# Attention in a fused decoder layer: first scores between the halves of the last projection, softplus ahead of the output's parts

## The chip, the core and the metric

The kernel runs on one core of a Trainium2 chip, as one launch. The time is device microseconds of one execution; before the change the median of three runs is 1053.36 us (1053.25 to 1054.24). In the tables and texts PE is TensorE (matmuls), PEld its weight loads, DVE is VectorE, ACT is ScalarE and SP is SyncE, which issues the DMAs. Every engine takes its own instructions in order and meets the others through semaphores.

## The reference

One decoder layer over 512 tokens of 1024 values, all in float32: a first SwiGLU, the token mixer, a second SwiGLU, a gated per-layer embedding, each with its norms. The change is in the mixer:

```
proj = h @ w_in
# eight stick-breaking heads
z = q k^T / 8
log_1m_beta = where(causal, log_sigmoid(-z), 0)
tail = reverse exclusive cumsum of log_1m_beta over the keys
a = where(causal, exp(log_sigmoid(z) + tail), 0);  o_sb = a v
# eight forgetting heads
logits = q k^T / 8 + F[t] - F[s], causal;  w = softmax(logits);  o_fx = w v
merged = concat(rms_norm(o_sb), rms_norm(o_fx))
out = merged @ w_out
```

## The kernel before

Each float32 operand is split into a rounded high part (made by ACT, `_hi`) and a rest (made by DVE as value minus high part, `_lo`), and a product is three matmuls: `product`, lines 1758 to 1760.

The mixer works in four tiles. Tile j holds one stick-breaking head pair and one forgetting head pair; each half-tile `hh` computes one head of each kind, number `hd = 2j + hh`. Tiles 0 to 2 are one loop body (`more` true), tile 3 is written out after it (`more` false). While tile j is computed, TensorE also projects the six columns (q, k, v of both kinds) of tile j + 1: `project(0)`, `project(1)`, `project(2)` in each half-tile, each in two weight units of twelve matmuls. All of them accumulate in one PSUM bank, `G_BANK` (bank 4). DVE empties it with `project_out` into `hold` (line 1427), and the next `project` waits for that (`hold_ready`). The second half-tile's `project(2)` is the last one of the tile.

A half-tile has, on TensorE: `first_logits` (lines 2064 to 2071) into banks 5 and 6; in the first half `v_transpose(0)` and `v_transpose(1)` (line 2019, four transposes each, into banks 7 and 3); the triangular sums on `sp_r`, 20 matmuls (line 2100), which wait for `sp_lo`; the last logits block `logits(1)`, which waits for the first softmax exponential (`p_exp`), since it reuses bank 5; `weigh(0)` (line 2115), the weights' transposes (line 2133), `weigh(1)`. `first_scores` (lines 2010 and 2013) computes z of the head that comes next.

From z, `softplus` goes three times over (ACT Abs, Exp, Ln; DVE line 1447), then ACT rounds (line 853) and DVE takes the rest (line 1453), which gives `sp_lo`. `qk_split` makes high and low parts of q and k (ACT lines 833 and 834, DVE lines 1433 and 1436); SP doubles the k rows by a DMA after it, and `first_scores` waits for that. `v_split` rounds v out of banks 7 and 3 (ACT line 838, DVE line 1441). `unit(x)` is one weight unit's split in the loop (ACT line 611, DVE line 1110); in tile 3 it is `part_out`: tile 3 has no projection of a next tile and instead multiplies the output weights with the three finished tiles, eight rows r of the output in `parts(x)`. Row r = 0 and row r = 2 both go through bank 4: row 2 waits until row 0 is out of it (`BANK4_FREE`, semaphore `part_lo`, ACT line 895 and DVE line 1508). Row 1 goes through bank 7 and waits for `v_split` to have read it.

`out_copy` and `out_sum` put the two halves of a head's output together (lines 942 and 1570), `out_hi` and `out_lo` round it and add its square (lines 949, 952, 1577, 1142).

The order on each engine is written by hand, in `mixer_tile` of each engine.

Of the kernel before, what the change touches and what calls it, by code (L numbers as in the profile page):

```python
# [32 lines left out]
TILES = HEADS // 2  # L33
# [146 lines left out]
def build(nc, t, out):  # L180
# [7 lines left out]
    with ExitStack() as ctx:  # L188
# [411 lines left out]
        def _(act):  # L600
# [235 lines left out]
            def v_split(tile, kind):  # L836
                act.wait_ge(v_t, 2 * tile + kind + 1)
                act.activation(v_r[kind][:, :, :, 0, :], v_source(kind), ACT.Copy).then_inc(v_hi, 1)
# [48 lines left out]
            def mixer_tile(j, more):  # L887
                for hh in range(2):
                    hd = 2 * j + hh

                    def part_out(x):
                        for r, b in zip(PART_AT[hh][x // 2], PART_BANKS[hh][x // 2]):
                            if r < EVICTED:
                                act.wait_ge(w_used, U_OUT + r + 1)
                                act.activation(xg[:, 0, PART_ROW[r], :], bank[b][:, :], ACT.Copy).then_inc(part_hi, 1)
                            if (hh, x) != (1, 2):
                                ahead(U_OUT, 0, 0, r)

                    def unit(x):
                        if more:  # L900
                            ahead(U_MIX + TILE_UNITS, j, TILE_UNITS, 6 * hh + x)
                        elif x % 2 == 0:
                            part_out(x)

                    def softmax_exp(i, b):
                        lb, at, w = L_AT[b]
                        src = L_BANKS[lb % 2][:, at:at + w]
                        first = 512 * lb + at

                        act.wait_ge(neg_max, 4 * hd + (1, 3, 3, 4)[i])  # L910
                        act.activation(pr[:, first:first + w], src, ACT.Exp, bias=stat[:, 0, b:b + 1],
                                       accum_out=stat[:, 1, b:b + 1]).then_inc(p_exp, 1)
                    if hh == 0:
                        v_split(j, 0)
                        v_split(j, 1)
                        if not more:
                            unit(0)
                    for i, b in enumerate((3, 2, 0)):
                        softmax_exp(i, b)
                    if hh == 1 and more:  # L920
                        unit(0)
                        unit(1)
                    act.wait_ge(tri_done, hd + 1)
                    for b in range(3):
                        c = slice(512 * b, 512 * b + Z_W[b])
                        act.activation(el[:, c], Z[b][:, 0:Z_W[b]], ACT.Exp).then_inc(a_exp, 1)
                        act.wait_ge(a_exp, 3 * hd + b + 2)
                        act.activation(sp_r[0][:, c], el[:, c], ACT.Copy).then_inc(a_hi, 1)
                    softmax_exp(3, 1)
                    if hh == 0 and more:  # L930
                        unit(0)
                        unit(1)
                    if hh == 1 and not more:
                        unit(0)
                    unit(2)
                    unit(3)
                    if hh == 1 and more:
                        qk_split(j + 1, 0)

                    def out_copy(kind):  # L940
                        act.wait_ge(o_done, 2 * hd + kind + 2)
                        act.activation(o_sum[halves[hh], kind, :], O_BANK[halves[0], :], ACT.Copy).then_inc(o_half, 1)

                    def out_hi(kind, gain):
                        if hh == 0:
                            return
                        act.wait_ge(o_added, 2 * hd + kind + 2)
                        g = gains[:, ds(GAIN_AT[gain] + j, 1)]
                        act.activation(oT[0][:, ds(j + 4 * kind, 1), :], o_sum[:, kind, :].unsqueeze(1), ACT.Copy,
                                       scale=g).then_inc(o_hi, 1)  # L950
                        act.wait_ge(added, ADD_AT[N_SB] + 2 * j + kind)
                        act.activation(o_sq, o_sum[:, kind, :], ACT.Square).then_inc(squared, 1)
                    out_copy(0)
                    for b in range(3):
                        c = slice(512 * b, 512 * b + Z_W[b])
                        act.wait_ge(pt_done, 3 * hd + b + 1)
                        act.activation(pt_r[0][:, c], PT_BANKS[b][:, 0:Z_W[b]],
                                       ACT.Copy).then_inc(pt_hi, 1)
                    if hh == 0:
                        softplus(hd + 1)  # L960
                        unit(4)
                        unit(5)
                        out_copy(1)
                    else:
                        if more:
                            qk_split(j + 1, 1)
                            unit(4)
                        out_hi(0, "sb_group_g")
                        if not more:
                            for r in PART_AT[1][1] + PART_AT[1][2]:  # L970
                                ahead(U_OUT, 0, 0, r)
                        unit(5)
                        out_copy(1)
                        if more:
                            softplus(hd + 1)
                        out_hi(1, "fox_group_g")


# [127 lines left out]
        def _(dve):  # L1106
# [392 lines left out]
            def mixer_tile(j, more):  # L1499
                for hh in range(2):  # L1500
# [38 lines left out]
                        dve.tensor_scalar(pr[:, c], pr[:, c], stat[:, 2, b:b + 1], None, MUL).then_inc(p_scaled, 1)  # L1539
                    if hh == 0:  # L1540
                        v_split(j, 0)
                        v_split(j, 1)
                        if not more:
                            unit(0)
                    for i, b in enumerate((3, 2, 0)):
                        normalise(i, b)
                    if hh == 1 and more:
# [4 lines left out]
                    for b in range(3):  # L1552
                        c = slice(512 * b, 512 * b + Z_W[b])
                        dve.wait_ge(a_hi, 3 * hd + b + 1)
                        dve.tensor_tensor(sp_r[1][:, c], el[:, c], plain(sp_r[0][:, c]), SUB).then_inc(a_lo, 1)
                    normalise(3, 1)
                    if hh == 0 and more:
                        unit(0)
                        unit(1)
                    if hh == 1 and not more:  # L1560
                        unit(0)
                    unit(2)
                    project_out(1)
                    unit(3)
                    if hh == 1 and more:
                        qk_split(j + 1, 0)

                    def out_sum(kind):
                        dve.wait_ge(o_half, 2 * hd + kind + 1)
# [17 lines left out]
                    if hh == 0:  # L1587
# [5 lines left out]
                        unit(4)  # L1593
                        unit(5)
                        out_sum(1)
                    else:
                        if more:
                            qk_split(j + 1, 1)
                            unit(4)
                        project_out(2)  # L1600
                        out_lo(0, "sb_group_g")
                        if not more:
                            for r in PART_AT[1][1] + PART_AT[1][2]:
                                ahead(U_OUT, 0, 0, r)
                        unit(5)
                        out_sum(1)
                        if more:
                            for b in range(3):
                                softplus(hd + 1, b)
                            softplus_lo(hd + 1)  # L1610
                        out_lo(1, "fox_group_g")


# [141 lines left out]
        def _(pe):  # L1755
# [266 lines left out]
            def mixer_tile(j, more):  # L2022
                for hh in range(2):
# [16 lines left out]
                    def parts(x):  # L2040
                        if more:
                            return
                        for r, b in zip(PART_AT[hh][x], PART_BANKS[hh][x]):
                            pe.wait_ge(w_lo, U_OUT + r + 1)
                            if b == 7:
                                pe.wait_ge(v_lo, 2 * TILES)
                            if b == 0:
                                pe.wait_ge(a_exp, 3 * hd + 2)
                            if r == 0:
# [30 lines left out]
                    if not more:  # L2080
                        first_logits()
                    project(0)
                    parts(0)
                    if more:
                        first_logits()
                    if hh == 0:
                        pe.wait_ge(hold_ready, 6 * j + 4)
                        pe.wait_ge(o_added, 2 * hd + 1)
                        v_transpose(0)
                        v_transpose(1)  # L2090

                    pe.wait_ge(sp_lo, 3 * hd + 3)
                    for c in range(TB):
                        b, at, w = Z_AT[c]
                        for jc in range(c, TB):
# [3 lines left out]
                            for part in range(2):  # L2099
                                last = pe.matmul(Z[b][:, off:off + jw], lhs, sp_r[part][:, 512 * jb + jat:512 * jb + jat + jw],  # L2100
                                                 start=False, stop=(jc == TB - 1 and part == 1), skip_group_check=True)
                    last.then_inc(tri_done, 1)

                    pe.wait_ge(p_exp, 4 * hd + 1)
                    logits(1).then_inc(l_done, 1)
                    project(1)
                    parts(1)

# [26 lines left out]
                        last.then_inc(pt_done, 1)  # L2135
                    if hh == 0:
                        first_scores(j, 1)
                    project(2)
                    parts(2)
                    pe.wait_ge(pt_lo, 3 * hd + 3)  # L2140
                    pe.wait_ge(o_added, 2 * hd + 2)
                    weigh(1, pt_r)
                    if hh == 1 and more:
                        first_scores(j + 1, 0)

            pe.wait_ge(consts, 1)
            keep_busy(14, bank[0])
# [149 lines left out]
```

## Time and profile before

| | us |
|---|---|
| median of three runs | 1053.36 |
| lowest, highest | 1053.25, 1054.24 |
| the profiled execution | 1053.56 |
| its span | 1051.7 |
| PE busy (with modelled ends) | 1038.6 |
| DVE busy | 785.5 |
| ACT busy | 558.4 |
| tiles 0 to 3 in the span | about 398 to 599 |

The profile is one execution. The gap of 1.9 us between its own time and its span lies outside the span. Matmuls overlap, so TensorE's cost is read best from start to start, and idle time in front of an instruction stands in square brackets with what ended it. The mean granted TensorE clock of the execution is 0.997 of full speed.

### The profile page before, as it was taken

To read this page: it belongs to the slowest core of one execution; us is meant where nothing else is said; L and a number is where in the kernel's file an instruction comes from. 1 tells how busy PE (TensorE), PEld (TensorE's weight loads), DVE (VectorE), ACT (ScalarE), POOL (GpSimd) and SP (SyncE) were. 2 spreads that over 40 slices of the span, in tenths; PEclk is the share of its full clock that TensorE was granted. 3 is DMA by queue.
4 is the path that set the end of the run, shared out by engine and by line. 5 is a ranking of instruction groups with operands and counts; after the bars stand their busy time and mean duration, and the time that the engine had idled before them with its cause. 6 is when DMAs were issued, how large, how long until landed. Compare 5 with 4: busy or idle time off the path is not lost.

```text
span 1051.7 us, 16615 instructions
## 1 busy us (share of the span) xinstructions
PE 1038.6 (99%) x6118; PEld 923.7 (88%) x6118; DVE 785.5 (75%) x1107; ACT 558.4 (53%) x922; POOL 10.0 (1%) x33
## 2 busy tenths in 40 slices
PE   9999999999999999999999999999999999999997
PEld 7889999998888878888888888889999998888886
DVE  6889888864343789796969889899888865454655
ACT  6634444343333558686869846544444344344645
POOL 1000000000002000000000000000000000000000
PEclk9999999999999999999999999999999999999999
DMA  6353423303323233232312122263423305444002
GB/s 213 94 175 106 135 81 106 98 21 111 95 94 100 61 100 90 62 88 58 85 51 61 56 85 81 83 188 108 134 81 105 97 21 162 144 135 159 1 21 80
DMA packets 99948, 100.59 MB, mean 96 GB/s; under 512 B 6672, under 2 KB 82192, under 8 KB 99888
## 3 DMA queue, kind: packets, MB, share of 16 engines
q1 hardware_dynamic: 99472, 99.47, 31.2%
q8 instruction: 40, 0.66, 0.3%
q10 hardware_dynamic: 416, 0.30, 0.1%
q14 instruction: 20, 0.16, 0.1%
HBM read 94.44 MB, written 2.10 MB: 92 GB/s over the span
## 4 chain that ended last, share of the span: by engine, by line
PE 87%; DVE 6%; ACT 4%; issue 2%; DMA 0%; DVEq 0%; ACTq 0%
PE bank L1758 27%; PE bank L1759 27%; PE bank L1760 27%; PE bank L2100 2%; DVE w_r L1110 1%; PE bank L2115 1%; DVE scratch L1656 1%; ACT scratch L847 0%; DVE big L1436 0%; DVE big L1453 0%; PE bank L2064 0%; ACT scratch L845 0%; DVE big L1433 0%; DMA gains<-in_gains 0%; DVE acc L1130 0%
## 5 line engine op out<-in xcount | busy, mean ns | idle before, releaser
L1110 DVE TENSOR_TENSOR w_r<-w_raw,w_r 128x512 fp32r<-128x512 f32 x204 | 138.0, 688 | 134.2 <-ACT w_r L611 128.6
L1758 PE MATMUL bank<-big,w_r 128*128 128x512 f32 (+1 forms) x676 | 236.1, 349 | 0.1
L1759 PE MATMUL bank<-big,w_r 128*128 128x512 f32 (+1 forms) x676 | 235.1, 348 | 0.0
L1760 PE MATMUL bank<-big,w_r 128*128 128x512 f32 (+1 forms) x676 | 235.0, 348 | 0.0
L611 ACT ACTIVATE w_r<-w_raw 128x512 fp32r<-128x512 f32 x204 | 125.3, 627 | 182.4 <-PE bank L1760 179.1
L1758 PE MATMUL bank<-big,xg 128*128 128x256 f32 (+1 forms) x728 | 214.2, 294 | 0.0
L1760 PE MATMUL bank<-big,xg 128*128 128x256 f32 (+1 forms) x728 | 213.7, 294 | 0.0
L1759 PE MATMUL bank<-big,xg 128*128 128x256 f32 (+1 forms) x728 | 213.7, 293 | 0.0
L666 ACT ACTIVATE xg<-over 128x1024 fp32r<-128x1024 f32 x72 | 75.4, 1055 | 143.4 <-DVE over L1199 90.0
L1758 PE MATMUL bank<-xg,w_r 128*128 128x512 f32 x378 | 150.1, 397 | 0.6 <-DVE scratch L1427 0.6
L1759 PE MATMUL bank<-xg,w_r 128*128 128x512 f32 x378 | 147.4, 390 | 0.0
L1760 PE MATMUL bank<-xg,w_r 128*128 128x512 f32 x378 | 147.3, 390 | 0.0
L1758 PEld LDWEIGHTS bank<-big,w_r 128*128 128x128 f32 x676 | 128.0, 189 | 17.0 <-DVE big L1577 0.6
L1760 PEld LDWEIGHTS bank<-big,w_r 128*128 128x128 f32 x676 | 128.0, 189 | 16.1
L1759 PEld LDWEIGHTS bank<-big,w_r 128*128 128x128 f32 x676 | 128.0, 189 | 15.9 <-issue 0.2
L1760 PEld LDWEIGHTS bank<-big,xg 128*128 128x128 f32 x728 | 139.5, 192 | 2.9
L1759 PEld LDWEIGHTS bank<-big,xg 128*128 128x128 f32 x728 | 139.5, 192 | 2.8
L1758 PEld LDWEIGHTS bank<-big,xg 128*128 128x128 f32 x728 | 139.5, 192 | 2.8
L1193 DVE TENSOR_TENSOR xg<-over,xg 128x1024 fp32r<-128x1024 f32 x72 | 88.0, 1223 | 16.5 <-ACT xg L666 16.1
L1758 PEld LDWEIGHTS bank<-xg,w_r 128*128 128x128 f32 x378 | 71.0, 188 | 17.1 <-issue 1.4
L1760 PEld LDWEIGHTS bank<-xg,w_r 128*128 128x128 f32 x378 | 71.0, 188 | 15.1
L1759 PEld LDWEIGHTS bank<-xg,w_r 128*128 128x128 f32 x378 | 71.0, 188 | 14.6 <-issue 0.7
(204 smaller groups left out, 1270.1 us busy)
## 6 DMA issues: line engine op xcount, KB each, us to landing
w_raw<-in_ffn_w_down SPq DMA_DIRECT2D x88, 256.0 KB, 2.7
over<-in_ffn_w_gate SPq DMA_DIRECT2D x24, 512.0 KB, 4.1
over<-in_ffn_w_up SPq DMA_DIRECT2D x24, 512.0 KB, 5.4
w_raw<-in_w_in SPq DMA_DIRECT2D x36, 256.0 KB, 3.1
w_raw<-in_ffn_w_up SPq DMA_DIRECT2D x24, 256.0 KB, 2.8
w_raw<-in_ffn_w_gate SPq DMA_DIRECT2D x23, 256.0 KB, 2.8
w_raw<-in_ffn_w_up SPq DMA_DIRECT2D x8, 512.0 KB, 5.8
w_raw<-in_ffn_w_gate SPq DMA_DIRECT2D x8, 512.0 KB, 6.8
```

Source lines behind the costliest of these rows:

```text
L611: act.activation(w_slot(0, slot, 0, 4 * P), w_raw[:, slot, :], ACT.Copy).then_inc(w_hi, 1)
L666: act.activation(ring[0][place], raw_set[q % 2][BLOCK_RAW[k]], ACT.Copy).then_inc(block_hi, 1)
L1110: dve.tensor_tensor(w_slot(1, slot, 0, 4 * P), w_raw[:, slot, :], plain(w_slot(0, slot, 0, 4 * P)), SUB).then_inc(w_lo, 1)
L1193: dve.tensor_tensor(ring[1][place], raw_set[q % 2][BLOCK_RAW[k]], plain(ring[0][place]), SUB).then_inc(block_lo, 1)
L1656: dve.tensor_tensor(gu[2 * a + half][:, c], src[:, c], rms[:, half, c], MUL).then_inc(y_half, 1)
L1758: pe.matmul(dst, w_hi_ap, m_hi, start=start, stop=False, skip_group_check=True)
L1759: pe.matmul(dst, w_lo_ap, m_hi, start=False, stop=False, skip_group_check=True)
L1760: return pe.matmul(dst, w_hi_ap, m_lo, start=False, stop=stop, skip_group_check=True)
L2100: last = pe.matmul(Z[b][:, off:off + jw], lhs, sp_r[part][:, 512 * jb + jat:512 * jb + jat + jw], start=False, stop=(jc == TB - 1 and part ...
L2115: last = pe.matmul(O_BANK[:, c * P:SEQ], v, a[part][:, first:first + w], start=c == 0 and part == 0, stop=c == TB - 1 and part == 1, skip_ ...
```

## The change

TensorE, in the loop's second half-tile: the next tile's `first_scores` moves from behind `weigh(1)` to between the two units of `project(2)`. In every first half-tile `v_transpose(1)`, with its wait for the previous output, moves from in front of the triangular sums to behind `logits(1)`. In tile 3's first half `parts(0)` moves from in front of the sums to behind them, and row 1 waits for one `v_split` fewer.

ACT and DVE, in the loop's second half-tile: `qk_split(j + 1, 0)` moves in front of `unit(3)`, on DVE also in front of `project_out(1)`. The next head's `softplus` moves in front of `unit(4)`, `out_copy(1)` or `out_sum(1)`, and both of `out_hi` or `out_lo`; `project_out(2)` goes between the second and third of its blocks on DVE. In every first half-tile `v_split(j, 1)` moves from the front to behind the softmax's last block, and in tile 3 `unit(0)` (row 0's eviction) moves there too, behind it.

```diff
@@ ScalarE (in VectorE the same, with normalise for softmax_exp) @@
                     if hh == 0:
                         v_split(j, 0)
-                        v_split(j, 1)
-                        if not more:
-                            unit(0)
                     for i, b in enumerate((3, 2, 0)):
                         softmax_exp(i, b)
...
                     softmax_exp(3, 1)
+                    if hh == 0:
+                        v_split(j, 1)
                     if hh == 0 and more:
                         unit(0)
                         unit(1)
-                    if hh == 1 and not more:
+                    if not more:
                         unit(0)
                     unit(2)
-                    unit(3)
                     if hh == 1 and more:
                         qk_split(j + 1, 0)
+                    unit(3)
...
+                    elif more:
+                        qk_split(j + 1, 1)
+                        softplus(hd + 1)
+                        unit(4)
+                        out_copy(1)
+                        out_hi(0, "sb_group_g")
+                        unit(5)
+                        out_hi(1, "fox_group_g")
@@ VectorE @@
                     unit(2)
+                    if hh == 1 and more:
+                        qk_split(j + 1, 0)
                     project_out(1)
                     unit(3)
-                    if hh == 1 and more:
-                        qk_split(j + 1, 0)
...
+                    elif more:
+                        qk_split(j + 1, 1)
+                        softplus(hd + 1, 0)
+                        softplus(hd + 1, 1)
+                        project_out(2)
+                        softplus(hd + 1, 2)
+                        softplus_lo(hd + 1)
+                        unit(4)
+                        out_sum(1)
+                        out_lo(0, "sb_group_g")
+                        unit(5)
+                        out_lo(1, "fox_group_g")
@@ TensorE @@
                             if b == 7:
-                                pe.wait_ge(v_lo, 2 * TILES)
+                                pe.wait_ge(v_lo, 2 * TILES - 1)
...
                     project(0)
-                    parts(0)
+                    if hh == 1:
+                        parts(0)
                     if more:
                         first_logits()
                     if hh == 0:
                         pe.wait_ge(hold_ready, 6 * j + 4)
-                        pe.wait_ge(o_added, 2 * hd + 1)
                         v_transpose(0)
-                        v_transpose(1)
...
                     last.then_inc(tri_done, 1)
+                    if hh == 0:
+                        parts(0)
                     pe.wait_ge(p_exp, 4 * hd + 1)
                     logits(1).then_inc(l_done, 1)
+                    if hh == 0:
+                        pe.wait_ge(o_added, 2 * hd + 1)
+                        v_transpose(1)
                     project(1)
                     parts(1)
...
-                    project(2)
+                    project(2, (0,))
+                    if hh == 1 and more:
+                        first_scores(j + 1, 0)
+                    project(2, (1,))
                     parts(2)
                     pe.wait_ge(pt_lo, 3 * hd + 3)
                     pe.wait_ge(o_added, 2 * hd + 2)
                     weigh(1, pt_r)
-                    if hh == 1 and more:
-                        first_scores(j + 1, 0)
```

VectorE in the loop's second half-tile, from the split of unit 2 on. `scratch<-bank,rms` is `project_out(1)`, the 64x512 rows are `qk_split(j + 1, 0)`; ISA and REGISTER_ALU rows compute what the next instruction waits for. This is VectorE there in the kernel before:

```order
L1110 TENSOR_TENSOR w_r<-w_raw,w_r 128x512
L1427 SCALAR_TENSOR_TENSOR scratch<-bank,rms 128x512
L1109 REGISTER_ALU
L1110 TENSOR_TENSOR w_r<-w_raw,w_r 128x512
L1432 ISA
L1433 TENSOR_TENSOR big<-scratch,big 64x512
L1435 REGISTER_ALU
L1436 TENSOR_TENSOR big<-scratch,big 64x512
L1432 REGISTER_ALU
L1433 TENSOR_TENSOR big<-scratch,big 64x512
L1435 REGISTER_ALU
L1436 TENSOR_TENSOR big<-scratch,big 64x512
```

And this is VectorE at the same place in the changed kernel:

```order
L1111 TENSOR_TENSOR w_r<-w_raw,w_r 128x512
L1433 ISA
L1434 TENSOR_TENSOR big<-scratch,big 64x512
L1436 REGISTER_ALU
L1437 TENSOR_TENSOR big<-scratch,big 64x512
L1433 REGISTER_ALU
L1434 TENSOR_TENSOR big<-scratch,big 64x512
L1436 REGISTER_ALU
L1437 TENSOR_TENSOR big<-scratch,big 64x512
L1428 SCALAR_TENSOR_TENSOR scratch<-bank,rms 128x512
L1110 REGISTER_ALU
L1111 TENSOR_TENSOR w_r<-w_raw,w_r 128x512
```

The four 64x512 subtractions now stand in front of the instruction that empties bank 4.

TensorE at the end of the loop's second half-tile. `bank<-xg,w_r` is the projection, `bank<-big` with 512, 384, 256 and 128 columns in turn is `weigh(1)`, the rows with `const_r` between them are the masks of `first_scores`. This is TensorE there before, from the projection's last matmul on:

```order
L1760 MATMUL bank<-xg,w_r 128x512
L2141 REGISTER_ALU
L2115 MATMUL bank<-big 128x512 x2
L2115 MATMUL bank<-big 128x384 x2
L2115 MATMUL bank<-big 128x256 x2
L2115 MATMUL bank<-big 128x128 x2
L2002 ISA
L2003 ISA
L2004 ISA
L2010 MATMUL bank<-big 128x512 x2
L2013 MATMUL bank<-const_r 128x128
L2010 MATMUL bank<-big 128x128 x2
```

And this is TensorE there in the changed kernel, from the first scores to the first three matmuls of the projection's second unit:

```order
L2013 MATMUL bank<-big 128x512 x2
L2016 MATMUL bank<-const_r 128x128
L2013 MATMUL bank<-big 128x128 x2
L2013 MATMUL bank<-big 128x384 x2
L2016 MATMUL bank<-const_r 128x256
L2013 MATMUL bank<-big 128x256 x2
L2016 MATMUL bank<-const_r 128x128
L2034 REGISTER_ALU
L1761 MATMUL bank<-xg,w_r 128x512
L1762 MATMUL bank<-xg,w_r 128x512
L1763 MATMUL bank<-xg,w_r 128x512
```

The scores stood behind `weigh(1)`, at the end of the body; they are now followed by twelve projection matmuls, `weigh(1)` and the branch.

ScalarE at the start of tile 3. `big<-bank 128x8x64` is `v_split`, `xg<-bank` is the eviction of an output row (row 0 first), the `scratch,stat` rows are the softmax. This is ScalarE there before:

```order
L838 ACTIVATE big<-bank 128x8x64 x2
L895 ACTIVATE xg<-bank 128x512
L611 ACTIVATE w_r<-w_raw 128x512
L911 ACTIVATE scratch,stat<-bank,stat 128x512
L911 ACTIVATE scratch,stat<-bank,stat 128x384
L911 ACTIVATE scratch,stat<-bank,stat 128x128
L926 ACTIVATE scratch<-bank 128x512
L928 ACTIVATE big<-scratch 128x512
L926 ACTIVATE scratch<-bank 128x512
L928 ACTIVATE big<-scratch 128x512
L926 ACTIVATE scratch<-bank 128x256
L928 ACTIVATE big<-scratch 128x256
```

And this is ScalarE there in the changed kernel, from the softmax's third block on:

```order
L911 ACTIVATE scratch,stat<-bank,stat 128x384
L911 ACTIVATE scratch,stat<-bank,stat 128x128
L923 ACTIVATE scratch<-bank 128x512
L925 ACTIVATE big<-scratch 128x512
L923 ACTIVATE scratch<-bank 128x512
L925 ACTIVATE big<-scratch 128x512
L923 ACTIVATE scratch<-bank 128x256
L925 ACTIVATE big<-scratch 128x256
L911 ACTIVATE scratch,stat<-bank,stat 128x256
L838 ACTIVATE big<-bank 128x8x64
L895 ACTIVATE xg<-bank 128x512
L611 ACTIVATE w_r<-w_raw 128x512
```

Row 0's eviction stood in front of the softmax; it now stands behind its last block and behind the second `v_split`.

## Rows read from the trace of the kernel before

**Rows 1.** waits, 400 to 600 us: waiter, releaser, total, times, longest
```profile
PE bank L2100 <- DVE big L1453: 3.3, 2, 2.3
PE bank L1758 <- DVE scratch L1427: 0.6, 2, 0.3
```

**Rows 2.** timeline, TensorE, tiles 1 and 2: start, us, engine, line, operation
```profile
453.03 0.50 PE L1758 MATMUL bank<-xg,w_r 128*128 128x512 f32 x1 [0.28 <-DVE scratch L1427]
...
497.62 0.48 PE L1758 MATMUL bank<-xg,w_r 128*128 128x512 f32 x1
503.17 1.37 PE L2115 MATMUL bank<-big 128*128 128x512 f32 x8
504.38 0.67 PE L2010 MATMUL bank<-big 128*128 128x512 f32 x2
506.43 0.50 PE L1758 MATMUL bank<-xg,w_r 128*128 128x512 f32 x1 [0.28 <-DVE scratch L1427]
525.00 0.71 PE L2010 MATMUL bank<-big 128*128 128x512 f32 x2
526.65 0.45 PE L1758 MATMUL bank<-xg,w_r 128*128 128x512 f32 x1
```

**Rows 3.** timeline, VectorE, tile 1's second half: units, splits, eviction
```profile
493.88 0.69 DVE L1110 TENSOR_TENSOR w_r<-w_raw,w_r 128x512 fp32r<-128x512 f32 x1
496.24 0.69 DVE L1110 TENSOR_TENSOR w_r<-w_raw,w_r 128x512 fp32r<-128x512 f32 x1
496.96 0.69 DVE L1433 TENSOR_TENSOR big<-scratch,big 64x512 fp32r<-64x512 f32 x1
505.08 0.69 DVE L1110 TENSOR_TENSOR w_r<-w_raw,w_r 128x512 fp32r<-128x512 f32 x1
505.69 0.68 DVE L1427 SCALAR_TENSOR_TENSOR scratch<-bank,rms 128x512 f32<-128x512 f32 x1
```

**Rows 4.** DMA view: destination, source, queue, count, size, us to landing
```profile
big<-big SPq DMA_DIRECT2D x24, 128.0 KB, 2.2
```

**Rows 5.** timeline, ScalarE: two steps of a softplus; another one's first
```profile
525.88 0.60 ACT L845 ACTIVATE scratch<-bank 128x512 f32<-128x512 f32 x1
528.99 0.63 ACT L849 ACTIVATE scratch<-scratch 128x512 f32<-128x512 f32 x1
...
558.99 0.60 ACT L845 ACTIVATE scratch<-bank 128x512 f32<-128x512 f32 x1
```

**Rows 6.** timeline of TensorE, tile 0, first half, after the sums
```profile
410.04 0.39 PE L2064 MATMUL bank<-big 128*128 128x256 f32 x1 [0.22 <-ACT scratch L911]
410.44 0.45 PE L1758 MATMUL bank<-xg,w_r 128*128 128x512 f32 x1
```

**Rows 7.** timeline of TensorE, last tile, first half
```profile
562.76 1.04 PE L2019 MATMUL bank<-ident,scratch 128*128 128x128 f32 x8
566.13 4.48 PE L2100 MATMUL bank<-big,const_r 128*128 128x512 f32 x20 [2.33 <-DVE big L1453]
570.89 0.44 PE L1758 MATMUL bank<-big,w_r 128*128 128x512 f32 x1
575.02 1.37 PE L2115 MATMUL bank<-big 128*128 128x512 f32 x8
```

**Rows 8.** windows: stretch, busy time by engine, PEclk (granted clock), DMA share, GB/s
```profile
563.80:566.10 2.30, 0.00 (x1) 0.00 (x0) 2.05 (x4) 2.30 (x6) 0.00 (x0) 1.00 0.00 0
567.30:570.60 3.30, 3.30 (x17) 3.30 (x16) 3.30 (x8) 2.62 (x9) 0.00 (x0) 0.50 0.00 0
```

**Rows 9.** timelines, ScalarE and VectorE: softmax in tile 2, last tile's start
```profile
515.36 0.69 ACT L911 ACTIVATE scratch<-bank,stat 128x512 f32<-128x512 f32 x1 [0.34 <-DVE stat L1525]
520.58 0.62 ACT L611 ACTIVATE w_r<-w_raw 128x512 fp32r<-128x512 f32 x1
...
567.44 1.35 DVE L1525 TENSOR_REDUCE stat<-bank 128x1 f32<-128x512 f32 x3
569.89 0.68 DVE L1508 TENSOR_TENSOR xg<-bank,xg 128x512 fp32r<-128x512 f32 x1
```

More of the change, by code:

```diff
@@ L963, in mixer_tile @@
                         out_copy(1)
-                    else:
-                        if more:
-                            qk_split(j + 1, 1)
-                            unit(4)
+                    elif more:
[6 more added lines that the diff above has]
+                        out_hi(1, "fox_group_g")
+                    else:
                         out_hi(0, "sb_group_g")
-                        if not more:
-                            for r in PART_AT[1][1] + PART_AT[1][2]:
-                                ahead(U_OUT, 0, 0, r)
+                        for r in PART_AT[1][1] + PART_AT[1][2]:
+                            ahead(U_OUT, 0, 0, r)
                         unit(5)
                         out_copy(1)
-                        if more:
-                            softplus(hd + 1)
                         out_hi(1, "fox_group_g")
@@ L1541, in mixer_tile @@
                         v_split(j, 0)
-                        v_split(j, 1)
-                        if not more:
-                            unit(0)
                     for i, b in enumerate((3, 2, 0)):
@@ L1556, in mixer_tile @@
                     normalise(3, 1)
+                    if hh == 0:
+                        v_split(j, 1)
                     if hh == 0 and more:
@@ L1559, in mixer_tile @@
                         unit(1)
-                    if hh == 1 and not more:
+                    if not more:
                         unit(0)
                     unit(2)
+                    if hh == 1 and more:
+                        qk_split(j + 1, 0)
                     project_out(1)
                     unit(3)
-                    if hh == 1 and more:
-                        qk_split(j + 1, 0)
                     def out_sum(kind):
@@ L1595, in mixer_tile @@
                         out_sum(1)
-                    else:
[L1597 to L1600, printed above, removed]
+                    elif more:
[10 more added lines that the diff above has]
+                        out_lo(1, "fox_group_g")
+                    else:
                         out_lo(0, "sb_group_g")
-                        if not more:
-                            for r in PART_AT[1][1] + PART_AT[1][2]:
-                                ahead(U_OUT, 0, 0, r)
+                        for r in PART_AT[1][1] + PART_AT[1][2]:
+                            ahead(U_OUT, 0, 0, r)
                         unit(5)
                         out_sum(1)
[L1607 to L1610, printed above, removed]
                         out_lo(1, "fox_group_g")
@@ L2102, in mixer_tile @@
                     last.then_inc(tri_done, 1)
+                    if hh == 0:
+                        parts(0)
                     pe.wait_ge(p_exp, 4 * hd + 1)
                     logits(1).then_inc(l_done, 1)
+                    if hh == 0:
+                        pe.wait_ge(o_added, 2 * hd + 1)
+                        v_transpose(1)
                     project(1)
```

## Prediction

> **What bounds the kernel now.** I read the table of busy times first: TensorE is busy nearly the whole span, so only what it waits for, its clock and its own work can move the time. Then the waits between 400 and 600 us, where the mixer runs. TensorE waits there seldom [rows 1]: 3.3 us in two places for `sp_lo` in front of the triangular sums (1.0 in tile 0, 2.33 in tile 3), and twice 0.28 us at the start of a tile, for VectorE to empty bank 4. Then its timeline. Two loop bodies run 53.40 us apart, from 453.03 to 506.43, and apart from the 0.28 each one is solid matmuls [rows 2]. In tile 3 the sums begin at 566.13 after 2.33 us of nothing [rows 7], and the windows show what follows: 1.00 of the clock granted in the idle stretch, 0.50 from about 567.3 to 570.6, which is 1.2 GHz [rows 8]. Sums and `logits(1)` take 4.76 us there; some 3.4 us at half clock hold 1.7 us of loss, so 3.06 at full clock. The change aims at 2.33 + 1.7 = 4.0 us. The question is what it puts in other places.
>
> **Loop body, second half-tile.** All times are those of tile 1 before, shifted only where I say so. VectorE now does the four q and k subtractions before it empties bank 4. It starts unit 2's rest at 493.88. From a unit to a subtraction, and from one subtraction to the next, it takes 0.72 us start to start (496.24 to 496.96), so they start at 494.60, 495.32, 496.04 and 496.76. ScalarE's high parts are not late: 0.63 us or less each [rows 5], begun as its unit 2 ends. The eviction follows 0.61 later (as 505.08 to 505.69), at 497.37, and lasts 0.68 [rows 3]. TensorE goes on 0.06 after it (505.69 + 0.68 against 506.43): 498.11. Before, it began `project(2)` at 497.62, with no wait [rows 2, 3]. That is a new wait of 0.49 us per body, and what is queued behind it is all of `project(2)` and the scores. With 0.72 in place of 0.61 it is 0.60.
>
> Half of `project(2)` is (503.17 − 497.62) / 2 = 2.78 us, so the next tile's scores start at 500.89, 3.5 us earlier than 504.38. The k rows they wait for are split by about 496.1 and land 2.2 us after their issue [rows 4], so no DMA is in the way. ScalarE's softplus starts up to 0.88 after the scores (525.00 against 525.88), at 501.77, and its second Ln ends 3.11 + 0.63 later, at 505.51 [rows 2, 5]. VectorE takes block two at 505.55 and only then empties bank 4: start 506.16, end 506.84, TensorE 506.90. TensorE itself would be ready at 500.89 + 1.65 (scores, 525.00 to 526.65) + 2.78 + 1.21 (`weigh(1)`, 503.17 to 504.38) = 506.53 [rows 2]. So the old wait of 0.28 becomes 0.37, and the tile starts at 506.90 instead of 506.43: **+0.47 us**, after tile 0 and after tile 1. Bounds: −0.28 per body if neither eviction were late, +0.7 if every spacing is the long one.
>
> The later units, `out_sum(1)` and `out_lo` feed nothing that TensorE wants within 5 us: a unit is used one projection after its slot, and the output only behind the last tile. I cost them at nothing; uncovered, each would cost its 0.69.
>
> **First half-tiles.** `v_transpose(1)` changes its place, not its length, in tiles 1 and 2, where `v_split(1)` has 5.5 us of projection over it. In tile 0 TensorE already waits 1.0 us at the sums, which the transposes no longer shorten, and `logits(1)` still waits for its exponential until 410.04; the projection at 410.44 comes four transposes later, of 1.04 us for eight less their overlap [rows 6, 7]: **+0.40 us**. Bounds 0 and 0.52.
>
> **Tile 3.** Softplus starts at 501.77 + 53.40 = 555.17. In the kernel before, the sums start 7.14 us after the first step (558.99 to 566.13) [rows 5, 7]; the same again gives 562.31, 3.8 earlier. The logits there take 1.3 us: before, they began at 504.38 + 1.65 + 53.40 = 559.43 and the transposes at 562.76, with 2.06 of `parts(0)` between. So TensorE is free at 506.53 + 53.40 + 1.3 + 0.40 = 561.6: idle for 0.7 only [rows 2, 7], and the wait aimed at is nearly gone. Sums end at about 565.0. `parts(0)` takes nine matmuls, half of the 4.13 us between 570.89 and 575.02: 567.1 [rows 7].
>
> Now `logits(1)` needs the exponential. VectorE, after its last rest at 562.25, has seven instructions of the outputs and units at 0.61 to 0.72 each, 4.6 us, before the first maximum: 566.8, only 0.6 before the old 567.44. ScalarE follows 0.7 later at 567.5, and needs 0.69 and the reading of the sum: TensorE starts `logits(1)` at 568.3, after 1.2 us idle, `v_transpose(1)` at 568.7, row 1 at 569.1, done at 571.2 [rows 3, 9].
>
> Row 2 then needs bank 4, where row 0 lies. Row 0's eviction was done by 569.89 + 0.68 = 570.57; now it is behind the softmax: 5.22 us from the exponential to what follows the last block (515.36 to 520.58) gives 572.7, `v_split(1)` 0.5, ScalarE's eviction to 573.8, VectorE's split and eviction at 0.68 each to 574.6 [rows 9]. So row 2 starts at 574.65 after **3.5 us of idle**, and `weigh(0)` at 576.7, where it was 575.02: **+1.7 us**. Behind it everything waits for TensorE as before, so this shift stays. Bounds: −1.0 (the second v rest, done at 574.0, is the next thing `weigh(0)` waits for) and +2.3 (every step 0.1 longer).
>
> An idle stretch of 2.33 us cost 1.7 us at 1.2 GHz [rows 7, 8]; the one of 3.5 us should do so again. I take **+1.7 us**, bounds 0 and 3.4 (two such falls, the idle 1.2 us helping).
>
> The Trainium skill, "TensorE: Matmul & The Clock Gate", section "HAM oscillation — how this bites in real kernels", says that an engine that stood idle goes back to half rate, and that the next burst pays for it. This trace agrees, with 0.50 granted behind the idle stretch. By that rule the change only moves the penalty; without it the sum is 3.0.
>
> **Sum.** 0.40 + 0.47 + 0.47 + 1.7 + 1.7 = +4.7 us. On the profiled execution's 1053.56 (span 1051.7 and 1.9 around it) this is 1058.3, on the median of 1053.36 it is 1058.1. An execution like the profiled one differs from the median by 0.2, far less than the terms.
>
> **Rivals.**
> - *No fall of the clock.* Idle 3.5 us, but cut so that full speed stays: 1.0 us in tile 0 passed without it. Then +3.0: 1056.4. Against it: 2.33 us sufficed.
> - *Two falls*, since three stretches of idleness (0.7, 1.2, 3.5) lie within 14 us: +6.4, 1059.8. For it: they are close; against it: the clock was back after 3.4 us of work.
> - *Row 0's eviction isn't late, the loop's is.* If ScalarE and VectorE reach row 0 before TensorE has finished row 1, `weigh(0)` starts at 574.1, −1.0, and the bodies cost 1.34: +0.4, 1053.8, no change. Against it: ten instructions in order on ScalarE between the exponential and the eviction, 5.7 us, while TensorE has 2.9 us of work.
> - *Faster: the wait and its half clock go, nothing takes their place.* The mechanism is the earlier softplus alone: the sums start 3.8 earlier and the 1.7 us of half clock are saved. It decides from the point at which row 2 finds bank 4 empty and `weigh(0)` finds its inputs; its price is −4.0, 1049.4. Against it: the 1.7 us between maximum and exponential are hardly earlier than before.
> - *The change doesn't do what it says*: scores between the halves, but the copied k rows late. It would add idle there; 4.8 us between split and scores against 2.2 to land exclude it.
>
> **Chances.** Forecast 0.58, no fall 0.18, two falls 0.08, no change 0.10, faster 0.06. What a measurement of this kernel can tell from no change is 0.2%, 2.1 us. The first three are slower: 0.84; no change 0.10; faster 0.06. The range leaves out the last two and a little above: 1054.8 to 1060.0. The likeliest case alone is 1057.0 to 1059.2.
>
> **What would show it.** In each body of the new profile TensorE waits some 0.5 us in front of `project(2)` and some 0.4 at the tile's start, both released by line 1428 (the old 1427). In tile 3 the sums wait under 1 us, `logits(1)` about 1.2 for the exponential, and the second row of `parts(1)` about 3.5 for line 1509, with half clock behind it. I would be wrong if the rows of tile 3 after the sums show no idle above 1 us, or if the bodies stay 53.4 us apart.

## Result and the profile after

The changed kernel takes 1058.64 us (median of six executions), the kernel before 1053.49 beside it: ratio 1.0045, 95% interval 1.0034 to 1.0056. Forecast was 1058.1. Single executions stand far outside (5890.5 us of the changed kernel, 1460.1 of evict_both, 1713.5 of the kernel before), and the ratios leave them out. The profiled execution takes 1058.68, its span is 1056.7: 5.0 us more than before.

The waits between 400 and 606 us (waiter, releaser, total, times, longest) answer to [rows 1]:

```profile
PE bank L1761 <- DVE xg L1509: 3.2, 1, 3.2
...
PE bank L2102 <- DVE big L1454: 1.8, 2, 1.4
...
PE bank L2067 <- ACT scratch L911: 1.5, 3, 1.0
...
PE bank L1761 <- DVE scratch L1428: 1.1, 3, 0.4
```

One wait is new and larger than any before: 3.2 us in front of an output row of `parts`, released by line 1509, VectorE's half of row 0's eviction. The sums' longest wait is now tile 0's 1.4 us, where tile 3's was 2.33. The exponential's (line 911) and bank 4's (line 1428) have grown.

TensorE's timeline over the second loop body answers to [rows 2]:

```profile
454.18 0.50 PE L1761 MATMUL bank<-xg,w_r 128*128 128x512 f32 x1
...
499.30 0.50 PE L1761 MATMUL bank<-xg,w_r 128*128 128x512 f32 x1 [0.36 <-DVE scratch L1428]
...
502.16 0.61 PE L2013 MATMUL bank<-big 128*128 128x512 f32 x2
...
503.71 0.46 PE L1761 MATMUL bank<-xg,w_r 128*128 128x512 f32 x1
...
506.54 1.37 PE L2122 MATMUL bank<-big 128*128 128x512 f32 x8
507.99 0.50 PE L1761 MATMUL bank<-xg,w_r 128*128 128x512 f32 x1
```

The first scores stand at 502.16, inside the projection. `project(2)` at 499.30 has waited 0.36. The bodies are 507.99 − 454.18 = 53.81 us apart, where they were 53.40. At 507.99 no idle is marked, but `weigh(1)` begins at 506.54 and takes 1.21 [rows 2]: TensorE could have gone on at 507.75 and lost 0.24.

Read from start to start, as the prediction does, the tile's start to `project(2)` takes 45.12 us (454.18 to 499.30), where it took 44.59 (453.03 to 497.62): 0.53 more. From there to the next tile's start it takes 8.69, where it took 8.81: 0.12 less.

VectorE there, as [rows 3]:

```profile
494.96 0.69 DVE L1111 TENSOR_TENSOR w_r<-w_raw,w_r 128x512 fp32r<-128x512 f32 x1
495.69 0.69 DVE L1434 TENSOR_TENSOR big<-scratch,big 64x512 fp32r<-64x512 f32 x1
...
498.56 0.69 DVE L1428 SCALAR_TENSOR_TENSOR scratch<-bank,rms 128x512 f32<-128x512 f32 x1
...
506.65 0.69 DVE L1448 SCALAR_TENSOR_TENSOR scratch<-bank,scratch 128x512 f32<-128x512 f32 x1 [0.83 <-ACT scratch L849]
507.26 0.68 DVE L1428 SCALAR_TENSOR_TENSOR scratch<-bank,rms 128x512 f32<-128x512 f32 x1
```

The eviction of `project(1)` starts at 498.56, behind the four subtractions that begin at 495.69, and ends at 499.25, 0.05 before TensorE resumes. The eviction of `project(2)` (507.26) follows the softplus's second block at once, and that block had waited 0.83 for ScalarE.

Tile 3 on TensorE, as [rows 7]:

```profile
563.85 2.98 PE L2102 MATMUL bank<-big,const_r 128*128 128x512 f32 x20 [0.36 <-DVE big L1454]
...
569.97 0.38 PE L2067 MATMUL bank<-big 128*128 128x256 f32 x1 [1.02 <-ACT scratch L911]
...
576.25 0.47 PE L1761 MATMUL bank<-big,w_r 128*128 128x512 f32 x1 [3.19 <-DVE xg L1509]
...
579.10 2.25 PE L2122 MATMUL bank<-big 128*128 128x512 f32 x8
581.19 1.28 PE L2140 MATMUL bank<-ident,scratch 128*128 128x128 f32 x10
```

The sums wait 0.36, `logits(1)` 1.02, row 2 3.19. `weigh(0)` lasts 2.25 instead of 1.37. The windows show why, as [rows 8]:

```profile
574.00:576.00 2.00, 0.00 (x0) 0.00 (x0) 1.94 (x5) 2.00 (x6) 0.00 (x0) 1.00 0.00 0
578.00:581.00 3.00, 3.00 (x10) 2.52 (x9) 1.03 (x2) 1.11 (x2) 0.00 (x0) 0.50 0.27 86
581.00:583.00 2.00, 2.00 (x19) 1.91 (x18) 1.21 (x3) 1.61 (x4) 0.00 (x0) 1.00 0.24 66
```

While TensorE does nothing, 1.00 of the clock is granted. It falls to 0.50 (1.2 GHz) at about 577.6, some 1.3 us after row 2 has begun, and stays there until 581.

What keeps row 2, on ScalarE and VectorE (answers to [rows 9]):

```profile
569.14 0.69 ACT L911 ACTIVATE scratch<-bank,stat 128x512 f32<-128x512 f32 x1 [1.47 <-DVE stat L1526]
...
574.20 0.58 ACT L838 ACTIVATE big<-bank 128x512 fp32r<-128x512 f32 x1
574.68 0.59 ACT L895 ACTIVATE xg<-bank 128x512 fp32r<-128x512 f32 x1
...
568.41 1.35 DVE L1526 TENSOR_REDUCE stat<-bank 128x1 f32<-128x512 f32 x3
...
575.43 0.68 DVE L1509 TENSOR_TENSOR xg<-bank,xg 128x512 fp32r<-128x512 f32 x1
```

From the exponential at 569.14 it is 5.06 us to `v_split(1)`, then row 0's eviction on ScalarE (574.68) and on VectorE (575.43, ends 576.11), then row 2 at 576.25. In the kernel before, the same VectorE instruction stood at 569.89, before the softmax's blocks.

Tile 0, `logits(1)` and the projection after it, as [rows 6]:

```profile
410.30 0.39 PE L2067 MATMUL bank<-big 128*128 128x256 f32 x1 [0.23 <-ACT scratch L911]
...
411.07 0.47 PE L1761 MATMUL bank<-xg,w_r 128*128 128x512 f32 x1
```

The first is 0.26 later than before, since everything ahead of it was: the sixteen matmuls of line 1994 (1997 here), ahead of the first scores, start at 384.62 in the trace before and at 384.88 here, in code that the change doesn't touch. The projection is 0.63 later. So the four transposes cost 0.37.

The account in the profiled executions:

| stretch | before | after | more | forecast |
|---|---|---|---|---|
| up to `logits(1)` of tile 0 | 410.04 | 410.30 | 0.26 | 0 |
| to tile 0's next projection | 0.40 | 0.77 | 0.37 | 0.40 |
| rest of tile 0 | 42.59 | 43.11 | 0.52 | 0.47 |
| tile 1 | 53.40 | 53.81 | 0.41 | 0.47 |
| tile 2, and tile 3 to the transposes behind `weigh(0)` | 69.81 | 73.20 | 3.39 | 3.4 |

Together 4.95 of the 5.0. Of the last line, row 2, `weigh(0)` and the clock take 581.19 − 576.25 = 4.94 us, where the same work takes 2.06 + 1.21 at full clock: 1.67 is the new fall of the clock. The other 1.72 is the later start of `weigh(0)` that the new order brings, against a kernel before that had its own wait and its own fall.

That old fall cost less than its 1.7 us. Before the change VectorE makes the rests that `weigh(0)` needs as follows:

```profile
572.94 1.62 DVE L1555 TENSOR_TENSOR big<-scratch,big 128x512 fp32r<-128x512 f32 x3
```

They end at 574.56, after a queue in which no idle is marked from 566.84 on, and `weigh(0)` starts at 575.02 [rows 7]. Sums that ended 1.7 us sooner would have let it start at most some 0.46 sooner (an estimate from these rows). The executions agree: a stretch of 3.3 us at 0.50 takes the mean clock of 1051.7 us down to 0.998, so the two executions of the kernel before at a mean of 1.000 did not have it, and they took 1053.34 and 1053.54, as long as the others. None of its executions on record is under 1052.93.

### The profile page after: what moved, and what is told of

Same layout as the page of the kernel before. It is cut to its first block, busy times and chain, and to the rows that moved or that the text cites. A ratio compares the mean times of both kernels' runs of the same rounds, so it can differ in the third digit from the quotient of the medians.

```text
span 1056.7 us, 16614 instructions
## 1 busy us (share of the span) xinstructions
PE 1040.0 (98%) x6118; PEld 923.2 (87%) x6118; DVE 786.0 (74%) x1107; ACT 558.5 (53%) x922; POOL 10.0 (1%) x33
## 4 chain that ended last, share of the span: by engine, by line
PE 85%; DVE 6%; ACT 6%; issue 3%; DMA 0%; ACTq 0%; DVEq 0%
PE bank L1761 27%; PE bank L1763 27%; PE bank L1762 27%; PE bank L2122 1%; DVE w_r L1111 1%; DVE scratch L1659 1%; DVE scratch L1428 1%; ACT scratch L847 1%; ACT scratch L845 1%; ACT w_r L611 1%; ACT scratch L911 1%; PE bank L2102 1%; ACT scratch L923 1%; PE bank L2013 1%; ACT scratch L849 0%
```

## Experiments

Each is an edit of the changed kernel. The medians (of 4 to 11 executions) stand beside 1053.46 to 1053.49 of the kernel before.

| kernel | us | ratio to before, interval |
|---|---|---|
| changed | 1058.64 | 1.0045, 1.0034 to 1.0056 |
| evict_first | 1059.14 | 1.0050, 1.0037 to 1.0063 |
| evict_both | 1056.82 | 1.0032, 1.0020 to 1.0044 |
| row0_early | 1055.19 | 1.0016, 1.0008 to 1.0025 |
| busy12 | 1057.24 | 1.0037, 1.0024 to 1.0050 |
| front_v | 1058.09 | 1.0044, 1.0028 to 1.0060 |
| old_tile3 | 1056.76 | 1.0030, 1.0020 to 1.0040 |
| both_row0 | 1053.10 | 0.9997, 0.9988 to 1.0006 |
| tight | 1052.31 | 0.9987, 0.9978 to 0.9996 |

**evict_first: is each late eviction a cost of its own?**

```diff
 # VectorE
+project_out(1)
 if hh == 1 and more:
     qk_split(j + 1, 0)
-project_out(1)
 unit(3)
```

> The changed kernel with one edit: in the loop's second half-tile VectorE empties bank 4 of project(1) before the four q and k rests, as in the kernel before. Theory (VectorE's order, both evictions together): the 0.36 us wait in front of project(2) goes, but the rests end 0.9 us later, so block two of the softplus starts at the same moment and project_out(2) behind it too; the wait at the tile's start grows from about 0.25 to 0.8 us. Body spacing stays 53.8 to 53.9 us, time 1058.4 to 1058.9, level with the changed kernel. Rival (each eviction's delay is its own cost): spacing 53.4, time 1057.6.

TensorE's timeline, the ends of that body:

```profile
499.15 0.48 PE L1761 MATMUL bank<-xg,w_r 128*128 128x512 f32 x1
...
506.36 1.37 PE L2122 MATMUL bank<-big 128*128 128x512 f32 x8
508.61 0.50 PE L1761 MATMUL bank<-xg,w_r 128*128 128x512 f32 x1 [0.88 <-DVE scratch L1428]
```

`project(2)` no longer waits, and the tile's start waits 0.88. With its start at 454.62 the body is 53.99 us, 0.18 longer than in the changed kernel. The time is 1059.14, 0.2 above what I expected and no gain. The theory stands: taking away the wait that the profile names first gives nothing, because VectorE's queue as a whole is late and the next eviction shows it.

**evict_both: both evictions in front**

```diff
 # VectorE, on top of evict_first
 elif more:
     qk_split(j + 1, 1)
+    project_out(2)
     softplus(hd + 1, 0)
     softplus(hd + 1, 1)
-    project_out(2)
```

> As evict_first, and project_out(2) also stands in front of the softplus's first block. Theory: both waits for line 1428 go, bodies 53.1 us apart (53.81 less 0.73), which is shorter than the 53.40 before; tile 3 begins 0.5 us earlier as well. Time 1056.5 to 1056.9. Rival (the bodies are longer because the scores in the middle or the transposes cost TensorE more themselves): spacing stays at 53.4 or above and the time above 1057.5.

TensorE's timeline, the same places:

```profile
453.20 0.44 PE L1761 MATMUL bank<-xg,w_r 128*128 128x512 f32 x1
...
497.67 0.48 PE L1761 MATMUL bank<-xg,w_r 128*128 128x512 f32 x1
...
504.89 1.37 PE L2122 MATMUL bank<-big 128*128 128x512 f32 x8
506.10 0.44 PE L1761 MATMUL bank<-xg,w_r 128*128 128x512 f32 x1
```

Both waits are gone, and the bodies are 506.10 − 453.20 = 52.90 us apart, 0.50 less than in the kernel before (0.30 expected). So the scores between the halves add nothing to TensorE's body; VectorE's order did. What the two bodies save is 1.8 us, and so is the time; tile 3's sums wait 0.98 in this trace instead of 0.36.

**row0_early: is bank 4 the gate of tile 3?**

```diff
 # ScalarE; the same on VectorE behind normalise
 for i, b in enumerate((3, 2, 0)):
     softmax_exp(i, b)
+if hh == 0 and not more:
+    unit(0)
...
-if not more:
+if hh == 1 and not more:
     unit(0)
```

> The changed kernel with one edit in tile 3's first half: row 0's eviction stands right behind the softmax's first three blocks on ScalarE and VectorE, instead of behind the last block and the second v split. Theory (bank 4 is the gate of row 2): row 2 follows row 1 without a wait, the 3.2 us of idle go; weigh(0) then waits for the v rest, which comes 1.05 us later than in the changed kernel, some 1.6 us of idle; it starts 2.5 us earlier than 579.1. Time 1056.1 if the clock stays, 1057.5 if it falls once more. Rival (the softmax chain is the gate, bank 4 only stands beside it): weigh(0) waits as long as row 2 did, time 1058.6 or more.

TensorE's timeline in tile 3:

```profile
569.95 0.38 PE L2071 MATMUL bank<-big 128*128 128x256 f32 x1 [1.02 <-ACT scratch L911]
...
576.65 1.47 PE L2126 MATMUL bank<-big 128*128 128x512 f32 x8 [1.55 <-DVE big L1444]
577.96 1.28 PE L2144 MATMUL bank<-ident,scratch 128*128 128x128 f32 x10
```

Row 2 has no wait left. `weigh(0)` waits 1.55 us for the v rest (1.6 expected) and starts at 576.65, 2.45 earlier. It lasts 1.47: no half clock follows in this trace, and the mean clocks of all eleven executions are 0.999 or 1.000. The time is 3.4 us lower, where I expected 2.5 without a fall. Only the part of the fall in front of `weigh(0)` (2.85 − 2.06 = 0.79 us) is in those 2.5; the 0.88 behind its start are saved too. Bank 4 was the gate.

**busy12: does the half clock come of the idle stretch?**

```diff
 # TensorE, tile 3's first half
 project(1)
+if hh == 0 and not more:
+    pe.wait_ge(v_lo, 2 * TILES - 1)
+    keep_busy(12, bank[7])
 parts(1)
```

> The changed kernel with 12 matmuls of ones by ones (128x128, about 3 us) into bank 7 before row 1 in tile 3's first half, so that TensorE is not idle while it waits for bank 4. They add nothing to the output. Theory (half clock comes of the idle stretch and costs 1.7 us): row 2 starts at the same time, no stretch at 0.50 behind it, time 1056.9. Rival (the half clock is not tied to that stretch): time 1058.6, with 0.50 granted from 577.8 to about 581.2 as now.

TensorE, and its windows (stretch, busy of PE, PEld, DVE, ACT, POOL, PEclk):

```profile
570.90 2.84 PE L1788 MATMUL bank<-ones 128*128 128x128 f32 x24
...
576.33 0.47 PE L1761 MATMUL bank<-big,w_r 128*128 128x512 f32 x1 [0.54 <-DVE xg L1509]
...
578.48 1.37 PE L2125 MATMUL bank<-big 128*128 128x512 f32 x8
```

```profile
571.00:573.50 2.50, 2.50 (x26) 2.50 (x24) 2.08 (x8) 2.40 (x5) 0.00 (x0) 1.00 0.02 7
576.00:580.00 4.00, 3.67 (x20) 3.24 (x21) 2.68 (x6) 2.19 (x5) 0.00 (x0) 1.00 0.22 68
```

Row 2 starts at 576.33, as before (576.25), and waits for the same line. But the clock stays at 1.00, and the transposes behind `weigh(0)` come at 579.69 instead of 581.19. That is 1.50 sooner, and the median falls by 1.4 us (1.7 expected). The half clock was the price of the idle stretch, apart from the stretch itself.

**front_v: the term of tile 0**

```diff
 # TensorE
     v_transpose(0)
+if hh == 0 and more:
+    pe.wait_ge(o_added, 2 * hd + 1)
+    v_transpose(1)
...
-if hh == 0:
+if hh == 0 and not more:
     pe.wait_ge(o_added, 2 * hd + 1)
     v_transpose(1)
```

> The changed kernel with one edit: in the loop bodies v_transpose(1) stands in front of the sums again (ScalarE and VectorE unchanged). Theory: in tile 0 the four transposes run in the wait for sp_lo again, so from the sums' start to the projection it takes 3.6 us as before the change and not 3.99; tiles 1 and 2 keep their length. Time 0.4 us under the changed kernel, 1058.2. Rival (the 0.4 us in tile 0 come from VectorE's later maximum): 3.99 stays and the time too.

From the sums' start (406.71) to the projection (410.32) it takes 3.61 us in its trace, in the changed kernel 3.99 (407.08 to 411.07). The tile 1 body keeps its length, 53.83 us. The trace shows the term; the medians' difference of 0.55 lies inside the intervals and shows nothing by itself.

**old_tile3: did tile 3's order have to follow the loop's?** Tile 3 is put back to its old order on three engines, under the new loop.

> The new loop with tile 3 in the old order (parts(0) and both transposes in front of the sums, row 0's eviction and both v splits in front of the softmax). Theory: parts(0) now waits for out_lo(0) of tile 2, which the new loop puts behind the softplus, until about 566.0; the sums start at about 568.8 instead of 563.9 and the clock falls, but rows 1 and 2 follow without a wait for bank 4, and weigh(0) starts at 577.8 instead of 579.1 with its clock penalty behind it. Time 1056.2 to 1056.8, below the changed kernel. Rival (tile 3 had to follow the new loop): the late parts(0) costs more than bank 4 does, time 1059 or more.

TensorE's timeline in tile 3 there:

```profile
566.53 0.47 PE L1767 MATMUL bank<-big,w_r 128*128 128x512 f32 x1 [3.01 <-DVE big L1583]
...
571.04 2.95 PE L2111 MATMUL bank<-big,const_r 128*128 128x512 f32 x20
...
578.34 1.37 PE L2129 MATMUL bank<-big 128*128 128x512 f32 x8
```

`parts(0)` waits 3.01 us for `out_lo(0)` of tile 2 (line 1583 there). The clock falls too: 0.58 in the mean from 567.5 to 570.9. I had expected the sums at 568.8 and they start at 571.04, mostly since `parts(0)` itself runs into the half clock (566.53 to 570.16, 3.63 us instead of 2.06). Still `weigh(0)` starts at 578.34 (577.8 expected), at full clock, and the median is 1.9 us under the changed kernel's. The rival falls: the loop's new order alone costs some 3.3 us, and the order that followed it in tile 3 another 1.9.

**both_row0 and tight: do the mends add, and how far do they go?** The first has the edits of evict_both and row0_early. The second adds front_v's and this in tile 3:

```diff
 # ScalarE; the same on VectorE
 if hh == 0 and not more:
-    unit(0)
+    part_out(0, split=False)   # row 0's eviction, its weight unit later
...
+if hh == 0 and not more:
+    v_split(j, 1)
 softmax_exp(3, 1)
```

> The edits of evict_both and row0_early together. Theory: the gains add, since the first is spent before tile 3's softmax chain starts and the second in it: 1055.2 less 1.9, so 1053.3, level with the kernel before. Rival (they hide one another): 1054.5 or more.

> both_row0 with v_transpose(1) in front in the loop bodies, and in tile 3's first half row 0's weight unit split later and v_split(1) in front of the softmax's last block, so that the v rest that weigh(0) waits for comes 1.15 us earlier. Theory: 0.4 and 1.15 us less than both_row0, 1051.7, faster than the kernel before by 1.8 us. Rival (the rest of the softmax becomes the new gate of weigh(0)): 1052.8.

The mends add: 1053.10 against the expected 1053.3. `tight` gains only 0.8 of the 1.55 expected. TensorE and ScalarE there:

```profile
573.17 1.46 PE L2133 MATMUL bank<-big 128*128 128x512 f32 x8 [0.58 <-DVE big L1446]
...
587.47 0.38 PE L2075 MATMUL bank<-big 128*128 128x256 f32 x1 [0.47 <-ACT scratch L911]
...
574.64 0.65 ACT L611 ACTIVATE w_r<-w_raw 128x512 fp32r<-128x512 f32 x1
575.16 0.59 ACT L945 ACTIVATE sq<-bank 64x512 f32<-64x512 f32 x1
```

`weigh(0)` starts at 573.17, 1.21 earlier than in both_row0 (574.38). But the next head's `logits(1)` comes 14.30 us after it, where it is 13.83 in both_row0. ScalarE now reaches `out_copy(0)` at 575.16 only, behind a weight unit, half a microsecond after `weigh(0)`'s last matmul; in both_row0 it had waited 0.37 for TensorE there and began at 575.89. So `weigh(0)` comes 1.21 sooner and the copy only 0.73, and the difference of 0.48 is what the next `logits(1)` is late by. The chain from the copy to that `logits(1)` is read from these two numbers; no run takes it apart. `tight` is 1.2 us faster than the kernel before; its interval lies below 1, though 0.13% is less than the 0.2% that I had named as the bound.

## Why the prediction was right

- *Loop bodies.* The step was VectorE's order against bank 4. It gave +0.47 a body, measured 0.52 and 0.41. The wait in front of `project(2)` was to add 0.49 start to start and added 0.53 in tile 1 (0.36 as marked idle). From there to the next tile's start 0.02 less was to come, and it was 0.12 less; the wait at the tile's start was to be 0.37 and is 0.24. `evict_first` shows that the two belong together, and `evict_both` that without them the body is shorter than before, so the moved scores are no term of the sum.
- *First half-tiles.* +0.40 in tile 0 alone, measured 0.37; `front_v` removes it. In tile 1 the move cost nothing: the body is 53.83 us in front_v and 53.81 here.
- *Tile 3.* The old wait shrank to 0.36 (0.7 forecast), the exponential's is 1.02 (1.2), bank 4's 3.19 (3.5). `row0_early` takes the last away and 3.4 us with it. The 3.8 us that the sums gained (563.85, less the 1.56 that tile 2 began later, against 566.13) were therefore real and spent on the waits behind them.
- *Clock.* 1.7 us forecast, 1.67 in the profile; `busy12` separates it from the wait. Here single executions differ: the changed kernel's are 1058.5 to 1058.7 at mean clocks of 0.998, one of 1056.87 at 0.999 and one of 1059.53 at 0.996. Those two stand near the rivals "no fall" and "two falls" (I said 1056.4 and 1059.8). In evict_first and evict_both, too, one execution at 0.999 lies under the median, by 2.1 and 1.8 us. That these are executions without the fall is likely and not shown: there is no trace of them, and the mean clock takes in the end of the span, after TensorE's last matmul, where the kernel before is at half clock a second time with no matmul left to slow (stretch, then busy PE, PEld, DVE, ACT, POOL, and PEclk):

```profile
1049.00:1050.00 1.00, 0.00 (x0) 0.00 (x0) 0.13 (x1) 0.00 (x0) 0.00 (x0) 0.50 0.78 287
```

- *The term that was mis-sized* is one that the sum doesn't use. The prediction has the old idle stretch cost 1.7 us of clock and the change aim at 4.0 us. The sums were that much longer, but VectorE's queue would have held `weigh(0)` until 574.56 without them too, so most of the 1.7 was covered; how much of the 2.33 in front of them was, no run shows. The price of −4.0 for "Faster" has the same fault; the best order tried, `tight`, is 1.2 us under the kernel before. The forecast stood, since it took `weigh(0)` from ScalarE's and VectorE's own chains and counted only the new fall, with nothing behind it to cover it. It took over the 1.7 without asking whether anything would cover it, and that nothing did is partly luck.
- *Rivals of the other sign.* "Faster" failed where I said it would, since row 2 didn't find bank 4 empty. "No change" needed ScalarE and VectorE to be early there.
- *The sum* is 0.3 to 0.5 short. 0.26 of it arose ahead of the mixer, in code that is the same. It is the spread of executions: over all ten traces the matmuls of line 1994 start between 384.42 (both_row0) and 385.36 us (old_tile3).

## What to carry to other kernels

When work is moved forward on the engines that feed a full TensorE, list what now stands behind it on each of them, above all the instruction that frees a shared PSUM bank: it belongs in front of any work whose result is needed later. Then ask of every wait what would hold the same consumer if it were gone. A wait that goes away in one place gives a gain only when the next consumer's own inputs are early too, so walk the queue on until TensorE runs without idleness again. After a few microseconds of idle TensorE, count a clock penalty beside the wait, but only as far as TensorE is what the next consumer waits for: where another engine's queue is as late, the slower matmuls are covered, and taking the penalty away gives little.

## What the runs showed of the hardware

- An idle stretch of 2.3 us (before), 3.2 (changed) and 3.0 (old_tile3) was followed by half clock, which made the matmuls behind it about 1.7 us longer. How much of that reached the kernel's time differed: 1.4 us in the changed kernel (busy12), and at most some 0.46 in the kernel before. In row0_early's trace, stretches of 1.0 and 1.55 us some 6 us apart did not bring it.
- Matmuls of 128x128 float32 ones kept the full clock as well as real work did (busy12).
- On VectorE inside the loop, the time from start to start hangs on what stands ahead of an instruction: 0.73 from 494.96 to 495.69, where a register is computed between the two, and 0.61 from 506.65 to 507.26, where none is (rows of the profile after). The subtractions over 64 partitions last 0.69, as long as the operations over 128.
